# Sixty exchanges of turned blocks moved from SP's queue to GpSimd's, in a two-layer float32 encoder

## The reference

```python
for i in range(2):
    u = rmsnorm(h, norm_mix[i])
    if i == 0:                       # conformer convolution module
        a = u @ w_pw1 + b_pw1;  val, gate = split(a)
        v = causal_depthwise_conv(val * sigmoid(gate), w_dw) + b_dw      # width 31
        m = silu(rmsnorm(v, g)) @ w_pw2 + b_pw2
    else:                            # short gated convolution
        b, c, v = split(u @ w_in)
        m = (b * causal_depthwise_conv(c * v, w_conv)) @ w_out           # width 3
    h = h + m
    h = h + square(relu(rmsnorm(h, norm_mlp[i]) @ w1[i])) @ w2[i]        # hidden 8192
    h = h + sigmoid(rmsnorm(h, norm_ple[i]) @ w_gate[i]) * (p[i] @ w_proj[i])
out = rmsnorm(h, norm_final)
```

## Time and profile before

| | |
|---|---|
| time, median of 3 runs | 2270.09 us (2269.92 to 2272.25) |
| the profiled execution | 2266.63 us, span 2264.9 us, granted PE clock 0.994 |
| PE busy | 2216.9 us, 98% |
| PEld busy | 1837.9 us, 81% |
| DVE busy | 1720.9 us, 76% |
| ACT busy | 1243.3 us, 55% |
| POOL busy | 156.9 us, 7% |
| SP's queue (q1) | 497600 packets, 499.71 MB, 71.3% of 16 engines |
| POOL's queue (q0) | 144 packets, 1.05 MB, 0.1% |

### The profile page before, as it was taken

One profiled execution on the slowest core, in us unless ns is written; L12 is line 12 of the kernel. 1 busy time (PEld: TensorE's weight loads), 2 busy tenths in 40 slices (PEclk: granted clock), 3 DMA queues, 4 the chain that ended last, 5 costly groups with the idle time before them and its releaser, 6 DMA issues.

```text
span 2264.9 us, 29438 instructions
## 1 busy us (share of the span) xinstructions
PE 2216.9 (98%) x10152; PEld 1837.9 (81%) x10152; DVE 1720.9 (76%) x1897; ACT 1243.3 (55%) x1542; POOL 156.9 (7%) x183
## 2 busy tenths in 40 slices
PE   8999999999999999999999999999999999999988
PEld 8998777888888888877788888878888888888766
DVE  6999868788788788667665667687887887886656
ACT  5666656556556556555544444555565564564545
POOL 3888000000000000000000000000000000000000
PEclk9999999999999999999999999999999999999989
DMA  9553598767768767588777777787687687685873
GB/s 342 162 164 135 168 299 256 232 204 240 228 201 240 233 196 239 167 259 251 228 237 215 220 250 219 248 257 220 208 239 225 207 241 228 204 240 156 272 250 112
DMA packets 499528, 503.56 MB, mean 222 GB/s; under 512 B 261040, under 2 KB 299120, under 8 KB 498416
## 3 DMA queue, kind: packets, MB, share of 16 engines
q1 hardware_dynamic: 497600, 499.71, 71.3%
q10 hardware_dynamic: 1696, 1.67, 0.2%
q0 software_dynamic: 144, 1.05, 0.1%
HBM read 464.62 MB, written 37.75 MB: 222 GB/s over the span
## 4 chain that ended last, share of the span: by engine, by line
PE 72%; DMA 5%; DVE 5%; ACT 2%; issue 1%; SPq 0%; DVEq 0%; ACTq 0%
PE acc L709 13%; PE acc L711 13%; PE acc L710 13%; PE acc L676 7%; PE acc L678 7%; PE acc L677 7%; PE tp L709 4%; PE tp L710 4%; PE tp L711 4%; DMA pl<-in_mlp_w 2%; DMA pT<-staged 2%; DVE wlo L1387 1%; DVE wlo L1557 1%; DVE prows L1471 1%; ACT whi L1042 1%
## 5 line engine op out<-in xcount | busy, mean ns | idle before, releaser
L1557 DVE TENSOR_TENSOR wlo<-pl,whi 128x1024 fp32r<-128x1024 f32 x372 | 443.7, 1207 | 153.5 <-ACT whi L1042 147.5
L1042 ACT ACTIVATE whi<-pl 128x1024 fp32r<-128x1024 f32 x372 | 386.9, 1049 | 307.7 <-PE acc L711 197.8
L1387 DVE TENSOR_TENSOR wlo<-raw,whi 128x1024 fp32r<-128x1024 f32 x248 | 296.2, 1221 | 141.7 <-ACT whi L937 133.0
L937 ACT ACTIVATE whi<-raw 128x1024 fp32r<-128x1024 f32 x248 | 256.3, 1054 | 209.1 <-PE acc L678 208.9
L1042 ACT ACTIVATE whi<-raw 128x1024 fp32r<-128x1024 f32 x196 | 207.5, 1059 | 186.0 <-PE acc L711 121.3
L1557 DVE TENSOR_TENSOR wlo<-raw,whi 128x1024 fp32r<-128x1024 f32 x196 | 239.3, 1221 | 54.9 <-ACT whi L1042 51.2
L676 PE MATMUL acc<-whi,b_hi 128*128 128x512 f32 x672 | 263.7, 392 | 7.8 <-DVE wlo L1387 7.8
L677 PE MATMUL acc<-wlo,b_hi 128*128 128x512 f32 x672 | 263.0, 391 | 0.0
L678 PE MATMUL acc<-whi,b_lo 128*128 128x512 f32 x672 | 262.9, 391 | 0.0
L709 PE MATMUL acc<-whi,a_hi 128*128 128x512 f32 x596 | 233.7, 392 | 8.1 <-DVE wlo L1557 8.1
L709 PE MATMUL acc<-whi,b_hi 128*128 128x512 f32 x596 | 232.8, 391 | 7.4 <-DVE wlo L1557 7.4
(11 more groups left out here) (218 smaller groups left out, 4044.3 us busy)
## 6 DMA issues: line engine op xcount, KB each, us to landing
pl<-in_mlp_w SPq DMA_DIRECT2D x368, 512.0 KB, 5.2
raw<-in_mlp_w SPq DMA_DIRECT2D x72, 1024.0 KB, 6.0
raw<-in_sc_w_in SPq DMA_DIRECT2D x48, 1024.0 KB, 5.7
raw<-in_cf_w_pw SPq DMA_DIRECT2D x64, 512.0 KB, 8.7
raw<-in_ple_w_gate SPq DMA_DIRECT2D x32, 1024.0 KB, 7.8
staged<-prows SPq DMA_DIRECT2D x240, 128.0 KB, 3.3
pT<-staged SPq DMA_DIRECT2D x56, 512.0 KB, 5.9
raw<-in_cf_w_pw SPq DMA_DIRECT2D x16, 1024.0 KB, 7.4
```

What stands on the lines that cost most here:

```text
L937: nc.scalar.activation(whi[:, e % SLOTS, :, :], raw[:, e // 2, 2 * (e % 2):2 * (e % 2) + 2, :], ACT.Copy).then_inc(hi_ready, 1)
L1042: nc.scalar.activation(whi[:, ring(parity, i), c, :], source[:, c, :], ACT.Copy).then_inc(slot_hi, 1)
L1387: nc.vector.tensor_tensor(wlo[:, e % SLOTS, :, :], raw[:, e // 2, 2 * (e % 2):2 * (e % 2) + 2, :], whi[:, e % SLOTS, :, :].bitcast(F32), A ...
L1557: nc.vector.tensor_tensor(wlo[:, ring(parity, i), c, :], source[:, c, :], whi[:, ring(parity, i), c, :].bitcast(F32), ALU.subtract).then_i ...
```

## The change

All sixty exchanges are taken out of SP's stream and written as one sequence on POOL: wait for the turn, wait until the exchange two before has come back, issue four transfers out, wait for their landing, wait for the operand where needed, issue the transfer back. The two buffers in HBM alternate by the exchange's number. SP keeps the weight loads, the stored embeddings and `gains`. The gate's first four weight tiles in a layer are asked for one step earlier. In layer 1 `gains` is asked for behind the second gate block's tiles and the embeddings, and DVE waits for it where it multiplies by it. In the ends of the layers on ACT and DVE, `keep`, `process`, `add_gated` and `turn` stand behind the split of their step instead of ahead of it, or a step apart from where they stood; in FIRST two slots change places.

```diff
-FIRST = (("m", 1, 0), ("d", 0, 0), ("m", 1, 1), ("d", 0, 1), ("m", 5, 0), ("d", 1, 0), ("m", 5, 1), ("d", 1, 1),
+FIRST = (("m", 1, 0), ("m", 1, 1), ("d", 0, 0), ("d", 0, 1), ("m", 5, 0), ("d", 1, 0), ("m", 5, 1), ("d", 1, 1),
-GATE_LOADS = (6, 8, 10, 12)
@@ SP @@
-            def stage_begin(T, rows=staged_rows):
-
-                sp.wait_ge(tr_ready, T + 1)
-                for i in range(TILES):
-                    nc.sync.dma_start(rows[:, :, i * Q:(i + 1) * Q], turned[i * Q:(i + 1) * Q, :, :]
-                                      ).then_inc(staged_ready, 16)
-            def take_back(r):
-
-                sp.wait_ge(staged_ready, 64 * r.T + 64)
-                sp.wait_ge(operand_ready, 2 * (r.o - 1) + 2)
-                nc.sync.dma_start(xt, staged_odd if r.j % 2 else staged).then_inc(xt_ready, 16)
...
@@ SP, load_step @@
-                    for f in fields if then is not END else ():
-                        field(layer, k + 1, f, free if f == fields[0] else None)
-                    if i == HIDDEN1 - 1:
-                        stage_early(c1)
-                    if i == HIDDEN1 + 3:
-                        take_back(c1)
-                    if i == hidden_before(t) - 1:
-                        stage_early(c0)
-                take_back(c0)
+                    for f in fields:
+                        if then is END:
+                            gate_tile(layer, f, free)
+                        else:
+                            field(layer, k + 1, f, free if f == fields[0] else None)
...
@@ DVE @@
+                    dve.wait_ge(final_ready, 16)
                     nc.vector.tensor_tensor(h[:, :, cols(r.j)], res[:, :, :],
                                             gains[:, cols(r.j)].unsqueeze(1).to_broadcast([P, 2, NB]), ALU.mult)
...
                 for e in range(HALVES):
+                    split_lo(g.b + 2, e)
                     if e == 1:
                         add_gated(o0)
-                        if layer == 0:
-                            turn(o0.T, o0.t)
-                    if e == 4:
+                    if e == 2 and layer == 0:
+                        turn(o0.T, o0.t)
+                    if e == 3:
                         add_gated(o1)
-                    split_lo(g.b + 2, e)
...
-            dve.wait_ge(final_ready, 16)
             run_gate(1, 1)
...
@@ POOL @@
+            def send(T):
+
+                pool.wait_ge(tr_ready, T + 1)
+                if T > 2:
+                    pool.wait_ge(*returned[T - 2])
+                for i in range(TILES):
+                    nc.gpsimd.dma_start((staged_rows, staged_odd_rows)[T % 2][:, :, i * Q:(i + 1) * Q],
+                                        turned[i * Q:(i + 1) * Q, :, :]).then_inc(staged_ready, 16)
+                pool.wait_ge(staged_ready, 64 * T)
+                return (staged, staged_odd)[T % 2]
+
+            def take_back(T, n, used=0):
+
+                sent = send(T)
+                if used:
+                    pool.wait_ge(operand_ready, used)
+                nc.gpsimd.dma_start(xt, sent).then_inc(xt_ready, 16)
+                returned[T] = xt_ready, 16 * n + 16
...
```

More of the change, by code:

```diff
@@ L417, in tile, with load @@
                 nc.sync.dma_start(raw[:, q, :, :], src).then_inc(raw_ready[q], 16)
-            def load(b, w, col, row=0, back=None):
+            def load(b, w, col, row=0):
                 for q in range(TILES):
@@ L463, in load_gate @@
             def load_gate(layer):
[L465 to L476, removed]
+                unit, w = gate[layer], t_in["ple_w_gate"][layer]
+                for q in range(TILES):
+                    tile(unit.b + 1, q, woven(w, TILES + q))
                 sp.wait_ge(slot_lo, freed(layer, STEPS, len(END) - 1))
@@ L480, in load_gate @@
                 nc.sync.dma_start(emb_in, emb_kept[:, layer, :, :]).then_inc(emb_back, 16)
-                tile(unit.b + 1, 3, woven(w, 7))
-                take_back(r3)
-                load(unit.b + 2, w, 2 * NB)
                 if layer:
[L485 to L492, removed]
+                    sp.wait_ge(slot_used, first_slot(layer, STEPS))
+                    nc.sync.dma_start(gains[:, :], t_in["norm_final"].partition_broadcast(P)).then_inc(final_ready, 16)
+                for j in (2, 3):
+                    load(unit.b + j, w, j * NB)
             def keep_emb(i):
@@ L506, in load_pw2 @@
                 for j in (2, 3):
-                    load(pw2.b + j, w, j * NB, back=exchange(Result(pw2, j - 2)))
+                    load(pw2.b + j, w, j * NB)
                     for i in range(BLOCKS):
@@ L642, in _ @@
             load_pw2()
[L643 removed]
+            load_mlp(0)
             load_gate(0)
[L645 to L653 removed]
+            with sp.Fori(1, BLOCKS + 1) as j:
+                load_win(j)
+            with sp.Fori(0, BLOCKS) as j:
+                load(wout.b + j, t_in["sc_w_out"][0], j * NB)
+            load_mlp(1)
             load_gate(1)
@@ L1084, in run_step @@
                             operand_hi(before[1].x, 2 * parity + 1, hid)
-                    if end:
-                        for j in range(3):
-                            if i == OUT_ADD[j]:
-                                keep(Result(down, j))
-                    else:
+                    if not end:
                         copy_product(t, base, i, 1, m1_copy, m1_copied)
@@ L1096, in run_step @@
                                plain_source(layer, k, t.load[i]), single)
+                    if end and i in OUT_ADD:
+                        keep(Result(down, OUT_ADD.index(i)))
                 if end:
@@ L1122, in run_gate @@
                 for e in range(HALVES):
+                    split_hi(g.b, e, LAYER * (layer + 1))
                     if e == 3:
                         keep(r3)
[L1125 to L1126 removed]
                         operand_hi(r1.x, 1, X[u], gain)
@@ L1606, in run_step @@
                             add_down(base + t.at("e", 3, 3) + 1, 3)
-                    if end:
-                        for j in range(3):
-                            if i == OUT_ADD[j]:
-                                process(Result(down, j))
-                        for j in range(2):
-                            if i == OUT_TURN[j]:
-                                turn(Result(down, j).T, Result(down, j).t)
-                    else:
+                    if not end:
                         for j in range(3):
@@ L1627, in run_step @@
                         weight_sum(t, n, later)
+                    if end and i in OUT_ADD:
+                        process(Result(down, OUT_ADD.index(i)))
+                    if end and i in OUT_TURN:
+                        r = Result(down, OUT_TURN.index(i))
+                        turn(r.T, r.t)
                 if end:
```

127 lines of the change are left out of this document (51 added, 76 removed).

## The result

Before 2270.01 us (2267.38 to 2272.25), after 2390.53 us (2387.71 to 2392.63): a ratio of 1.0531, 95% interval [1.0512, 1.0549]. The change costs 120 us where I had forecast 38. The direction was right, and the time lies near the upper end of the forecast's own range (2275 to 2400), but the size was wrong by a factor of three.

The account below looks back on a forecast made before the run. PE was taken as busy throughout the long stretches, its waits for weight splits capping gains near 32 us; 0 + 39 + 3 - 4.4 = +38 us gave 2308 us, 8-in-10 range 2256 to 2850 (forecast's own 2275 to 2400).

Parts of the forecast that it names:

- 5.7 us are absorbed: At the layer ends and in `w_in`: 5.7 us of an exchange's lateness never reach PE (ACT waited 9.10, PE stood 3.38).
- (a): Latency on POOL's queue: +1.7 us per dependent transfer, two in a row per exchange, +3.4 us.
- (b): POOL's issue of 1,024 short runs: 1.35 us each, +2.7 us for four; bounds 0 to +19.3 us.
- The 31 us: How much lower the forecast sum would be if many descriptors cost POOL little and issue stayed near its lower bound.
- the rival with the same issue time and the same relief: Faster rival: POOL's issue 0.69 us and the backlog goes; 2250 to 2264 us, centred at 2260; chance 27%.
- (c): Own queue for exchanges: passes SP's weight backlog but shares engines; half of 2.7 us returned, -1.35 us in a step.
- The steps: MLP steps: exchanges grow by 4.75 us to 16.7 and 16.6, within limits 18.2 and 16.9; 28 just fit, 0 us.
- The backlog: At the layer ends: ten of 18 exchanges exceed 9.1 us by 51 us together; half of that goes, -25 us.
- `gains`, -4.4: Layer 1 gate: the later wait for `gains` removes PE's longest wait, -4.4 us, between 0 and -6.1.
- Reordering: Layer ends and FIRST: moved additions and `keep` delay and advance by one split equally; 0 us, within +-12 together.
- SP alone on weights: SP no longer stands for turns, so weight tiles come earlier, but PE is full in those stretches: 0 us.
- The heavy rival: POOL pays per run: steps stall from 1.4 us per outgoing transfer; near 2500 to about 3200 us; chance 28%.

## Why the prediction was wrong in size

**The step that failed: "5.7 us are absorbed", at the ends and in `w_in`.** I read the 5.7 us from one exchange after layer 1 (ACT 9.10, PE 3.38) and set it for all 18 waits of ACT and the eight exchanges of `w_in`. Twelve of the 18 belong to `pw2`, the gate and `w_out`. For these twenty exchanges the 5.7 us made 114 us of cover, of which ACT's waits before had used 30, so I counted 84 as left. The pure delay measured 24. Stage by stage, in us of the span:

| | forecast | measured |
|---|---|---|
| `pw2`, gate, `w_out` (12 exchanges) | +35 | +76 |
| `w_in` (8) | +3 | +51 |
| the other six waits +29, relief of the backlog -25, `gains` -4 | 0 | -2 |

The worst term is `w_in`: +3 us, because an exchange without a wait seemed to have all 5.7 us free. With my own +6.1 us per exchange and 1.2 us absorbed, 20 x (6.1 - 1.2) = 98 us would have stood where I had 38. That the last row came out is luck: neither its 29 us nor its 25 us appeared.

The missing cover is in part idle time and in part the clock. PE's idle time rose by 87.3 us, 4.4 per exchange of 7.2 us of added length, so about 3 us are covered. Then 36.9 us of slower matmuls after the stalls, 1.8 per exchange, take back most of that. I gave the clock no price.

**The length at these places: 6.1 forecast, 7.2 measured, for other reasons.** (a) and (b), latency and issue, I had at 3.4 + 2.7 us. With SP held off, POOL's own surcharge in `w_out` is 1.6 us. The issue is 0.79 us, under the 1 to 1.7 us that I named as the test of the forecast, so by my own test the forecast failed there and the lower bound was nearly right. (The 31 us that I named for that bound don't follow from my rows; the rival with the same issue time and the same relief came out 44 us lower.) (c), the relief of an own queue, had the wrong sign outside the steps. I took it from the steps, where a block had 2.7 us of weights ahead of it. In `w_out` it had none, and a stream of its own adds 7.4 us of company there (10.0 against 6.4 us out, 7.3 against 3.5 back). The rows of before had the hint: ACT starts at 1414.17, and SP asks for that block at 1410.61, so this way back needs 3.6 us where the median is 5.9. I used the 9.1 us as the length of an exchange on any queue; it was that of a sheltered one.

**The steps, 0 forecast: right, with a surcharge of 4.75 us that came out at 0.8.** 16.7 us forecast, 13.3 measured (15.6 the longest), against limits of 18.2 and 16.9. Before, these blocks had their company on the way back (6.6 us), now on the way out. PE idles 2.4 of 570 us, all of it around the first hidden blocks and none in the repeated steps.

**The backlog, -25 forecast: it gave back almost nothing.** The 20 us exchange after layer 1 (19.9 us to its landing) takes 20.7 us after the change: the way back fell from 13.2 to 10.1 us, and the way out rose from 5.7 to 10.0. Its counterpart in layer 0 takes 19.0 us as before. So my test, a length below 14, came out on the forecast's side, but a queue of its own doesn't pass 2 MB that share its engines, and half of the backlog, which I took off, didn't go. Asking for the block first does, for 10.4 us.

**`gains`, -4.4: right** (-4.2 alone). The load itself lands after 15.9 us in the changed kernel, and nobody waits. **Reordering, 0 within 12: right by its bounds** (some +4 us alone, if the 4 us of `gains` add to it, and at most 11 more in the changed kernel). **SP alone on weights, 0 for PE: incomplete.** It gave PE nothing, and it was the source of the company.

**The heavy rival** fell with the issue of 0.79 us. The number of runs matters, but mostly while the transfer travels: 96 us in all, where the four issues became only 1.1 us shorter (3.1 against 2.0 us).

## What to carry to other kernels

Before a transfer is moved off a shared queue, ask what the queue was holding back for its sake: a stream in order is also a reservation of the DMA engines. Read the slack from the place that pays (here delays of 1.9 and 5.9 us in eighteen exchanges gave it in two runs), never from the place with the longest wait. Price PE's stalls together with the slower clock that follows them (here 37 us of slower matmuls beside 87 us of idle time), and look for one small block asked for behind megabytes: moving it ahead gained 10 us.

## What the chip showed unexpectedly

- POOL's issue of 1,024 runs of 128 bytes takes 0.79 us, against 0.56 for the 128-row way back and 0.49 for 32 runs of 4 KB. SP's takes 0.67, 0.34 and 0.42. Each grows by only 0.25 to 0.30 us between few runs and 1,024.
- The same four transfers of 128-byte runs take 5.5 us alone on SP, 6.4 us on POOL with the loads held back, and 10.0 us there beside 1 MB loads; a single 512 KB read takes 3.4, 3.5 and 7.3 us (`w_out`, means).
- POOL's queue shows 20368 packets for 64 MB with short runs or long. On SP the short runs were counted one by one: 261040 packets under 512 bytes before, 15280 once the exchanges had moved.
- Soon after a PE stall of 4.15 us, matmuls start every 0.43 us for 3.4 us.
- Transfers out with long runs took 4.4 us in `w_out` and 7.6 us in `w_in` on the same queue: 0.2 and 1.5 MB of other data moved beside them.
